# The 64 weight-sum steps of the pool layer's output, issued in the heads of the mLSTM layer

## The reference, cut to what matters

```python
for i in range(DEPTH):
    if i % 2 == 0:
        branch = _mlstm_branch(x, ..., mlstm_w_out[j])   # ends in (hb * silu(z)) @ w_out
    else:
        branch = _pool_branch(x, ..., pool_w_out[j])     # ends in (mixed * silu(z)) @ w_out
    x = _layer_norm(DEEPNORM_ALPHA * x + branch, post_ln_g[i], post_ln_b[i])
```

## Time and profile before

| | us |
|---|---|
| median of 3 runs | 1417.78 |
| lowest, highest | 1417.61, 1418.93 |
| profiled execution | 1417.28 |
| span of its instructions | 1415.4 |
| TensorE busy | 1394.5 |
| VectorE busy | 1143.7 |
| ScalarE busy | 804.0 |
| GpSimd busy (DMA issue not counted) | 152.2 |

### The profile page before, as it was taken

The page is one execution under the profiler, slowest core; times in us unless marked ns, Lnnn a source line. Parts: engine busy times, 40 slices in busy tenths (PEclk is TensorE's granted clock), DMA queues, the critical chain, the costliest instruction groups (busy, mean ns, idle before and its releaser), DMA issues.

```text
span 1415.4 us, 19382 instructions
## 1 busy us (share of the span) xinstructions
PE 1394.5 (99%) x6488; PEld 1155.0 (82%) x6488; DVE 1143.7 (81%) x1739; ACT 804.0 (57%) x1202; POOL 152.2 (11%) x251
## 2 busy tenths in 40 slices
PE   9999999999999999999999999999999999999997
PEld 7788888888888888888878888877888888888885
DVE  7978879788797978879764446897798888889976
ACT  6876757667675665767743346665344443436341
POOL 2001001110100101010000001001111111100011
PEclk9999999999999999999999999999999999999999
DMA  5023425343342524436487666444665556689651
GB/s 227 19 83 105 127 53 164 79 139 103 100 128 57 164 68 135 111 97 201 135 286 249 207 208 217 134 127 98 170 150 148 152 155 159 170 275 351 212 193 75
DMA packets 103441, 213.31 MB, mean 151 GB/s; under 512 B 10912, under 2 KB 27552, under 8 KB 102192
## 3 DMA queue, kind: packets, MB, share of 16 engines
q1 hardware_dynamic: 90544, 178.53, 37.8%
q0 software_dynamic: 12800, 33.56, 12.3%
HBM read 170.04 MB, written 75.56 MB: 174 GB/s over the span
## 4 chain that ended last, share of the span: by engine, by line
PE 72%; DVE 6%; ACT 2%; issue 1%; DMA 1%; POOL 0%; SPq 0%; DVEq 0%; ACTq 0%; POOLq 0%
PE wide L2767 16%; PE wide L2769 15%; PE wide L2768 15%; PE ps_state L2767 2%; PE ps_state L2768 2%; PE ps_state L2769 2%; PE ps_inter L2768 2%; PE ps_inter L2767 2%; PE ps_inter L2769 2%; PE ps_intra L2939 1%; PE ps_state L2945 1%; PE ps_intra L2942 1%; PE ps_s L2767 1%; PE ps_intra L2767 1%; PE ps_s L2768 1%
## 5 line engine op out<-in xcount | busy, mean ns | idle before, releaser
L2768 PE MATMUL wide<-xa,inb 128*128 128x512 f32 x576 | 225.0, 391 | 0.0
L2767 PE MATMUL wide<-xb,inb 128*128 128x512 f32 x472 | 190.4, 403 | 1.3 <-DVE inb L1877 0.3
L2769 PE MATMUL wide<-xb,inb 128*128 128x512 f32 x472 | 184.3, 390 | 0.0
L2768 PEld LDWEIGHTS wide<-xa,inb 128*128 128x128 f32 x576 | 108.8, 189 | 19.8
L2768 PE MATMUL wide<-xa,blk 128*128 128x512 f32 x320 | 124.5, 389 | 0.0
L2767 PEld LDWEIGHTS wide<-xb,inb 128*128 128x128 f32 x472 | 88.8, 188 | 22.5 <-issue 3.7
L2769 PEld LDWEIGHTS wide<-xb,inb 128*128 128x128 f32 x472 | 88.6, 188 | 18.9
L2767 PE MATMUL wide<-xb,blk 128*128 128x512 f32 x256 | 99.8, 390 | 1.2 <-ACT zz L1749 1.1
L2769 PE MATMUL wide<-xb,blk 128*128 128x512 f32 x256 | 99.6, 389 | 0.0
L1797 ACT ACTIVATE wy<-wy_raw 128x1024 fp32r<-128x1024 f32 x56 | 59.5, 1062 | 61.3 <-DMA wy_raw<-y_block 61.0
L2767 PE MATMUL wide<-xa,inb 128*128 128x512 f32 x208 | 83.8, 403 | 3.9 <-ACT z_buf L1176 2.7
(11 more groups left out here) (431 smaller groups left out, 3820.1 us busy)
## 6 DMA issues: line engine op xcount, KB each, us to landing
in_raw<-in_w_in SPq DMA_DIRECT2D x45, 512.0 KB, 4.2
wy_raw<-y_block SPq DMA_DIRECT2D x56, 256.0 KB, 4.3
mw_raw<-h_block SPq DMA_DIRECT2D x53, 256.0 KB, 3.3
m_sum<-in_w_out POOLq DMA_DIRECT2D x48, 256.0 KB, 4.3
h_block<-f_buf SPq DMA_DIRECT2D x48, 256.0 KB, 3.5
w_sum<-in_pool_w_out POOLq DMA_DIRECT2D x48, 256.0 KB, 4.2
a_raw<-in_pool_w_z SPq DMA_DIRECT2D x16, 512.0 KB, 4.0
a_raw<-folded SPq DMA_DIRECT2D x16, 512.0 KB, 4.5
```

The costliest lines, as they stand in the source:

```text
L2767: pe.matmul(dst, a[0], b[0], start=first, stop=False, skip_group_check=more)
L2768: pe.matmul(dst, a[0], b[1], start=False, stop=False, skip_group_check=more)
L2769: return pe.matmul(dst, a[1], b[0], start=False, stop=last, skip_group_check=more)
```

## The change

The 64 steps of the pool layer's weight are no longer issued behind `prod` but follow the first weight's 64 in the same places of the heads. To have room for 128 steps, one is due per 9/8 products in place of 9/4. The last of them is due one product ahead of the end of the heads' products. Nothing else is changed: same transfers, same number of them, same semaphores at the readers.

```diff
             def sums_until(tick):
-                while m_steps[0] < W_STEPS and W_TICK + m_steps[0] * 9 // 4 < tick:
-                    pool.wait_ge(in_prod, W_TICK + m_steps[0] * 9 // 4 + 1)
-                    sum_step(m_steps[0], w_out, m_sums, m_summed)
+                while m_steps[0] < 2 * W_STEPS and W_TICK + m_steps[0] * 9 // 8 < tick:
+                    pool.wait_ge(in_prod, W_TICK + m_steps[0] * 9 // 8 + 1)
+                    if m_steps[0] < W_STEPS:
+                        sum_step(m_steps[0], w_out, m_sums, m_summed)
+                    else:
+                        sum_step(m_steps[0] - W_STEPS, p_out, w_sums, w_summed)
                     m_steps[0] += 1
...
-            assert m_steps[0] == W_STEPS
+            assert m_steps[0] == 2 * W_STEPS
...
-            for n in range(W_STEPS):
-                pool.wait_ge(prod, 4 + n + n // 4)
-                sum_step(n, p_out, w_sums, w_summed)
```

## The result

| | before | after |
|---|---|---|
| median, us | 1418.36 (4 runs, 1417.61 to 1419.11) | 1442.2 (4 runs, 1439.1 to 1445.27) |
| ratio, 95% interval | | 1.0168 [1.0139, 1.0197] |
| profiled execution, us | 1417.28 | 1444.66 |
| its span, us | 1415.4 | 1442.8 |

The changed kernel is slower by 23.8 us. 1434 was forecast, with a range of 1417 to 1463. Its profiled execution lost 27.4 us; its four runs differ by 6 us, those of before by 1.5.

What follows compares the result with a forecast made beforehand. TensorE, busy 99% of the span, was taken as the bound. GpSimd's serial step chain at 4.6 us a step would make it late by 120 x 4.6 - 535.7 = +16 us, so 1417.8 + 16 = 1434 us, range 1417 to 1463.

Steps and rivals of the forecast that it cites:

- What is lost nothing for: Pool layer: its 64 steps hold up nobody on TensorE, so removing them there gives nothing.
- The rival that the pool layer's end gains: After 1262 us: output-stage loads land sooner without the last steps, at most 4 us faster, to 1414; chance 0.04.
- The chain and its readers: Heads: late steps delay GpSimd's ones (8.2 us cover) and first power (4.8); TensorE waits 0 to 3 us at a time.
- The formula: Mask of head 1 to ones of head 7: TensorE late by 120 c - 535.7 us, c the pace; zero at 4.46.
- The pace, 4.6: Heads: issue-to-issue time per step taken as 4.6 us, between estimates 4.64 and 4.46, giving +16 us.
- The clock, taken as full: Heads: TensorE's clock stays at 2.4 GHz through waits of 0 to 3 us; no loss.
- SyncE's loads, taken at nothing: Heads: input-weight loads up to 0.7 us later per head, taken as 0, with +5 us for the range.
- The fit of the Trainium skill: Any 256 KB step: 2.0 us plus bytes over 436 GB/s, so steps take about 3.3 us and always keep up; no change.
- The chain keeps up: Heads: rival that the pace stays under 4.48 us and cover takes every lag, 1417.8 us; chance 0.17.
- congests: Heads: rival that steps and SyncE's transfers lengthen each other, pace over 4.83 us, +44 to +87 us; chance 0.07.

Runs made afterwards that it cites:

- adds as copies: The changed kernel, one chain in the same places, with every adding step made a plain copy, sums left out: 1417.42 us, 0.9993.
- 5/4 products: The changed kernel at one step per 1.25 products, 115 steps in the heads and 13 in the pool layer: 1419.27 us, 1.0006.
- two chains: The changed kernel with the two weights' steps alternating in the same places, so two transfers can be in flight: 1425.93 us, 1.0057.
- two chains of copies: The changed kernel with the two weights' steps alternating and every add made a plain copy: 1420.44 us, 1.0007.
- ones by VectorE: The changed kernel with GpSimd's two memsets of ones per head moved to VectorE: 1436.89 us, 1.0132.
- two chains at 5/4: The changed kernel with alternating weights, one step per 1.25 products, the last 13 steps behind the heads' last power: 1445.46 us, 1.0184.

## Why the prediction was right, and where it was off

- *What is lost nothing for.* Right. The pool layer's steps hid behind full TensorE work; the rest of the program behind the heads is 0.8 us shorter, and with the heads undisturbed (adds as copies) the whole is 0.9 us shorter, within its interval. The rival that the pool layer's end gains falls.
- *The chain and its readers.* Right. Landings set the steps, the ones and the first power come late, TensorE waits on L2939, masks are 85.0 to 88.3 us apart. The experiments confirm it from three sides: a second transfer in flight, shorter landings, or a slower demand (5/4 products) each take these waits away, but for 0.9 us at the ones of head 7 in the last.
- *The formula.* Right, as far as it says that the last step sets the last wait. The last step was issued at 698.99, so the pace from 137.7 on was (698.99 - 137.7) / 120 = 4.68 us. 120 x 4.68 - 535.7 = 25.9 us, and 25.65 were measured. As this pace is read from the last step itself, the agreement confirms only the two ends (137.7, and 1.3 us from the last issue to TensorE), not the pace.
- *The pace, 4.6.* Mis-sized by 0.08, which is 10 us. The landings themselves are 4.05 us on average, with 0.52 from a landing to the next issue: 4.57, near what I took. The other 0.11 are for the most part pauses in which GpSimd waits for a product, a mask's row or a variance. I named those waits as a danger and then took the pace from a stretch that has none of them: it was a pace of steps, and the sum needed one of the queue. A second part is the last head, whose traffic I had not looked at; there SyncE loads the next stage's weights as well, and a step there took up to 7.7 us (673.03 to 680.75). Its eight intervals (658.03 to 698.99) took 5.12 us each and the 112 before them 4.65, which makes 3.8 of the 10 us.
- *The clock, taken as full.* Wrong, and the trace of before could have said so. It has a wait of 2.7 us in head 0, with matmuls on both sides, and behind it the clock is at half for 3.4 us (TensorE's waits and a window, kernel before):

```profile
PE wide L2767 <- ACT z_buf L1176: 2.7, 1, 2.7
...
63.70:67.10 3.40, 2.88 (x7) 2.33 (x8) 3.33 (x4) 3.23 (x6) 0.00 (x0) 0.50 0.50 164
```

  So "in full wherever it has matmuls" was a reading of the stretches that I had cut out. After the change it was at half for 3.4 us behind a wait of 2.3 us, and for 10.2 us (695.2 to 705.4) from the midst of the wait of 8.2 on; the matmuls in these 10.2 cost 2.5 us on the path. I had waits of 0 to 3 us in mind. What the shorter drop cost isn't shown: behind it TensorE may only have waited less, but GpSimd's chain also stood 3.5 us between a landing and the issue at 477.08, for a variance, which may itself come later when TensorE is late.
- *SyncE's loads, taken at nothing.* Right for one chain, by VectorE's waits for them (7.6 us for 7.9), though the loads landed later by 0.3 us in the median (4.5 for 4.2); with two in flight they were 19.1.
- *The fit of the Trainium skill* (page "DMA: Bandwidth & Descriptors", section on the anatomy of one DMA on the software path) gives an estimate of 2.6 us for 256 KB. It is near for a copy, 2.9 in the run, and short for an add, 4.4. Its result, no change, is what happened as soon as the adds were copies.
- *The rivals.* "The chain keeps up" failed by 0.2 us a step; "congests" was not reached, as the pace stayed below 4.83.

In the medians the loss is 23.8 us. With the same terms for the clock and the rest, the pace would be (23.8 - 2.5 + 0.8 + 535.7) / 120 = 4.65 us, an estimate. So of the 7.5 us between the 16.3 forecast and the 23.8 measured, 5.8 are the pace and 2.5 the clock, less 0.8 for the rest.

## What to carry to other kernels

Steps that wait for each other's landing on one queue have a pace. Compare it, pauses of the queue included, with the pace asked, and leave room (here 4.95 us asked was free and 4.70 was not, at a mean of 4.68), because one slow head is enough to use up the cover. Then look for the small operations behind the steps in the same queue: they carry the lag to the engine that bounds. Moving work from a stretch where it hid anyway has nothing to win. And before you take a clock as full, look in the trace for what it did behind the waits that are there already.

## What the runs showed of the hardware

- An adding transfer of 256 KB from device memory to device memory took 4.4 us in the median to land in the changed kernel, a copy 2.9; at 32 KB the add took 2.4.
- With two chains, in which two adds are often in flight together, SyncE's loads of 512 KB on another queue took up to 8.6 us to land (5.8 before) and VectorE's waits for them grew from 7.9 to 19.1 us; with two chains of copies it was 6.0 and 8.0.
- TensorE's granted clock was at 1.2 GHz for 3.4 us behind a stall of 2.68 us in the kernel before (from 63.7) and behind one of 2.3 us in the changed one (from 435.8). It fell within the stalls of 8.2 us (for 10.2 us in all) and, with 6.7 us of transposes just ahead, of 4.8 us (for 6.8 us).
- The length of a stall alone doesn't tell whether it falls: it stayed full behind stalls of 2.79 us (ones by VectorE, from 459.4) and 3.06 us (two chains at 5/4, from 488.6), and was at half for 3.4 us (from 7.9) behind one of 1.88 us, at the start of the program with one step per 5/4 products.
